# PEER decoder block: v rows half a block behind the u rows, two tokens in one product, and a block's last scaling one slot behind its sum and squares

## The chip, the cores and the metric

The kernel runs on one core of one Trainium2 chip, as one program. The metric is the device time of that program in microseconds (us), as a median of several runs; the kernel before takes 3320.57 us.

## What is computed

The reference is one decoder step for 1024 prompt tokens and 32 sample tokens of width 1024, all in float32. A first half mixes tokens (an input projection, causal pooling, a depthwise convolution of width 31, a LayerNorm, an output projection). The second half retrieves experts:

```python
q = (hf @ w_query).reshape(-1, PEER_HEADS, 2, PEER_HALF)
s = jnp.einsum('nhpk,hpmk->nhpm', q, sub_keys)
sv, si = lax.top_k(s, PEER_TOPK)                       # 16 of 128, twice a head
comb = sv[:, :, 0, :, None] + sv[:, :, 1, None, :]      # 256 pairs, the best 16 of them
fv, fpos = lax.top_k(comb.reshape(-1, 8, 256), PEER_TOPK)
...
a = jnp.einsum('phkd,pd->phk', u_table[ex], hx)        # 128 rows of u for every token
act = jax.nn.gelu(a, approximate=False) * gx
out = jnp.einsum('phk,phkd->pd', act, v_table[ex])     # 128 rows of v for every token
```

Each token takes 8 x 16 = 128 rows of `u_table` and the same 128 rows of `v_table`, 4 KB a row. For 1056 tokens that is 1109 MB of gathered rows. A residual add and a last RMSNorm follow.

## The kernel before

The tokens are 8 blocks of 128 and one of 32 (block `NB` = 8). The whole program is laid on a line of **slots**: (NB + 1) x 32 of them. In slot s = 32p + c, each engine's loop `for p ... for c ...` does chunk c of block p of the u part, chunk c of block p - 1 of the v part, and then the small steps that the table `steps[s]` names.

**The u part.** One u fetch is an indirect DMA issued by GpSimd (L783): pick k of all 128 tokens of the block, one row on each partition (512 KB). VectorE multiplies the row by the token and sums (L1337), one instruction of 1024 elements a fetch, four fetches a slot. The ring `u_ring` has NU = 6 places; a fetch waits until VectorE has freed its place (`u_free`). GpSimd also waits, each 32 picks, for `found`, the count of finished top-k searches (L777, inc at L1305).

**The v part.** One v fetch (L800) is the other way round: all 128 picks of one token, one on each partition. TensorE multiplies them (L1701) by a column of weights: `act_x` is a mostly zero buffer in which the weights of a token stand at such a distance that a window of 32 columns has them in the token's own row. The 128 tokens end up in the partitions of the two banks `acc`. Four v fetches a slot, ring `v_ring` with NV = 6 places, freed by TensorE (`v_free`). GpSimd issues in program order: four u fetches, then four v fetches, slot after slot.

**From u to v.** For the weights of a block all 128 picks must be done: VectorE `weigh(b)` multiplies gelu and gate to `act_w`, TensorE `weights(b)` transposes it (L1680), ScalarE `take_weights` copies it (L943), `spread` puts it into `act_x`, a quarter of the tokens at a time, and `tokens` (L1684) starts. This stands in slot 0 of the next block. The expert numbers are transposed likewise (`numbers`, `transposed_numbers`; table steps "turn", "turned"), once a block, since a v fetch needs all of a token's picks in one column. `finish(b)` (L1356) then scales the sums, adds y, squares and sums it (L1361 to L1366), waits for ScalarE's square root (L962) and scales (L1370), all in slot 0 of block b + 2.

**The table.** `lay_out()` (L157) fills `steps`: `fill` puts the token mixer and queries of the groups of blocks [2, 3, 4] and [5, 6, 7, 8] into slots by a list of costs (`COST`), from slot 5 on, up to a load per slot of 8 in block 0 and `ROOM` = 4.8 or 4.6 later; `spread` puts the pieces of the top-k searches. VectorE does a slot's steps one slot later (`DVE_LAG`). Group [0, 1] is worked ahead of slot 0. A step "xn" is `norm_x` (L1101) on VectorE, which waits for a square root by ScalarE (`x_root`, L835); "x" is the transposition on TensorE (`x_turned`, L1494), "in", "conv", "out", "q" are its products.

**Ends.** After slot 264 there is no u part; v fetches then use the places of both rings (`v_place`, `V_LAST`).

## Time and profile before

| | |
|---|---|
| three runs, us | 3320.57, 3324.29, 3314.8 |
| the profiled execution, us | 3321.2 |
| its span (first to last instruction), us | 3319.4 |
| mean granted TensorE clock, share of full | 0.82 |
| busy: TensorE / VectorE / ScalarE / GpSimd | 65% / 64% / 11% / 69% |
| moved by DMA | 1235.06 MB, 372 GB/s over the span |

The span is 1.8 us less than the execution's own time. A row of a timeline gives start, duration, engine, line, operation and tiles; in square brackets stands how long the engine had been idle and what ended that. A row of a table of stretches gives the stretch, its length, for each engine busy time and number of instructions, the granted clock, the DMA share and GB/s. CUSTOM_DVE_ANT_0 at L1337 is the u product; the trace's line numbers are those of the kernel before.

### The profile page before, as it was taken

What the parts mean: (1) busy time and instruction counts of PE and PEld (TensorE: products, weight loads), DVE (VectorE), ACT (ScalarE), POOL (GpSimd) and SP (SyncE); (2) the same over time, 40 slices, a digit from 0 to 9 for tenths busy, and PEclk for the clock granted to TensorE, in tenths of its full rate; (3) what the DMA queues carried; (4) which work ended last, traced back from release to release, by engine and by line L of the source; (5) the groups of instructions that cost most, each with busy time, mean ns of one, the idle gap of its engine ahead of it and who ended that gap; (6) DMA issues with size and microseconds to landing.
All of it is one profiled execution on the core that took longest, in us unless ns stands there. A gap on an engine that the chain in (4) does not pass through costs nothing.

```text
span 3319.4 us, 30349 instructions
## 1 busy us (share of the span) xinstructions
PE 2172.9 (65%) x9719; PEld 962.3 (29%) x9719; DVE 2132.8 (64%) x4860; ACT 360.3 (11%) x754; POOL 2284.6 (69%) x2229
## 2 busy tenths in 40 slices
PE   7884966567675588987564876674454445545576
PEld 5573532134331134542111443341111111111111
DVE  1577885767888557655756678777766666675301
ACT  2112340000001101321000000000000000000000
POOL 0144657677777777777767777777777777777675
PEclk9997988778887799999777887887666776786799
DMA  8778779999999999999999999999999999999998
GB/s 289 200 276 288 279 255 379 399 401 386 381 400 395 385 402 407 409 392 391 400 391 387 402 387 367 386 362 378 398 409 406 409 388 406 403 408 370 373 408 329
DMA packets 363454, 1235.06 MB, mean 372 GB/s; under 512 B 36856, under 2 KB 40336, under 8 KB 363280
## 3 DMA queue, kind: packets, MB, share of 16 engines
q0 software_dynamic: 304784, 1109.40, 86.7%
q1 hardware_dynamic: 36335, 79.69, 6.9%
q10 hardware_dynamic: 22176, 44.04, 3.5%
q8 instruction: 78, 1.28, 0.2%
q14 instruction: 81, 0.66, 0.1%
HBM read 1220.31 MB, written 13.28 MB: 372 GB/s over the span
## 4 chain that ended last, share of the span: by engine, by line
POOL 31%; DMA 26%; PE 22%; issue 11%; DVE 7%; DVEq 1%; ACT 1%; SPq 0%; POOLq 0%; ACTq 0%
DMA v_ring<-in_v_table_dram,eidt 19%; POOL u_ring L783 16%; POOL v_ring L800 14%; PE bank L1701 12%; DMA u_ring<-in_u_table_dram,eid 3%; PE bank L1520 3%; DVE u_ring L1337 2%; PE bank L1619 2%; PE bank L1537 2%; PE bank L1595 2%; DMA u_ring<-in_v_table_dram,eidt 1%; POOL u_ring L800 1%; DVE mixt L1176 1%; DMA wring<-in_w_in_dram 1%; DMA u_ring<-in_w_ada_dram 0%
## 5 line engine op out<-in xcount | busy, mean ns | idle before, releaser
L1701 PE MATMUL bank<-v_ring,act_x 128*32 128x512 f32 x3984 | 1165.9, 810 | 918.1 <-DMA v_ring<-in_v_table_dram,eidt 910.5
L1337 DVE CUSTOM_DVE_ANT_0 u_ring<-u_ring,h 128x1024 f32<-128x1024 f32 x1056 | 1278.4, 1225 | 745.3 <-DMA u_ring<-in_u_table_dram,eid 674.1
L783 POOL DMA_INDIRECT u_ring<-in_u_table_dram,eid x1024 | 1132.9, 1106 | 465.3 <-issue 302.8
L800 POOL DMA_INDIRECT v_ring<-in_v_table_dram,eidt x996 | 1041.4, 1046 | 392.0 <-issue 244.2
L1701 PEld LDWEIGHTS bank<-v_ring,act_x 128*32 128x32 f32 x3984 | 268.5, 135 | 1735.1 <-issue 1720.3
L1619 PEld LDWEIGHTS bank<-hbuf,wring 128*128 128x128 f32 x1984 | 230.1, 196 | 24.9 <-issue 24.9
L1619 PE MATMUL bank<-hbuf,wring 128*128 128x128 f32 (+1 forms) x1984 | 236.3, 280 | 0.0
L1537 PE MATMUL bank<-zc,dring 128*128 128x384 f32 x496 | 189.5, 508 | 7.7 <-ACT dring L832 7.7
L1520 PE MATMUL bank<-hbuf,wring 128*128 128x384 f32 (+2 forms) x448 | 151.4, 497 | 17.7 <-DMA wring<-in_w_in_dram 13.5
L1595 PE MATMUL bank<-wring,mixt 128*128 128x512 f32 (+1 forms) x256 | 125.0, 638 | 0.0
L1361 DVE TENSOR_TENSOR scratch<-bank,mod 128x512 f32<-128x512 f32 x18 | 11.6, 686 | 176.1 <-PE bank L1701 174.6
L1520 PEld LDWEIGHTS bank<-hbuf,wring 128*128 128x128 f32 x448 | 86.0, 195 | 85.4 <-issue 46.8
L1537 PEld LDWEIGHTS bank<-zc,dring 128*128 128x128 f32 x496 | 84.0, 190 | 55.4 <-issue 23.6
L832 ACT ACTIVATE dring<-ident,cw 128x128 f32<-128x128 f32 x248 | 78.4, 390 | 109.0 <-PE bank L1539 78.4
L1337 DVE DVE_READ_ACCUMULATOR2_ANT dot<- 128x1 f32 x1056 | 87.5, 83 | 0.0
L937 ACT ACTIVATE dot<-dot 128x32 f32<-128x32 f32 x33 | 7.6, 229 | 712.9 <-DVE dot L1337 696.3
L1701 PE MATMUL bank<-u_ring,act_x 128*32 128x512 f32 x240 | 57.3, 595 | 22.6 <-DMA u_ring<-in_v_table_dram,eidt 22.6
L800 POOL DMA_INDIRECT u_ring<-in_v_table_dram,eidt x60 | 56.2, 937 | 21.3 <-issue 15.6
L1595 PEld LDWEIGHTS bank<-wring,mixt 128*128 128x128 f32 (+1 forms) x256 | 47.0, 192 | 79.8 <-issue 79.8
L916 ACT ACTIVATE qt<-bank 128x512 f32<-128x512 f32 (+1 forms) x36 | 20.2, 562 | 366.6 <-PE bank L1619 366.6
L927 ACT ACT_TABLE_LOAD x32 | 41.1, 1283 | 166.5 <-PE bank L1595 92.1
L1539 PEld LDWEIGHTS bank<-zcs,dring 128*128 128x128 f32 x248 | 46.9, 189 | 33.1
(260 smaller groups left out, 1679.6 us busy)
## 6 DMA issues: line engine op xcount, KB each, us to landing
u_ring<-in_u_table_dram,eid POOLq DMA_INDIRECT x1024, 7.1
wring<-in_w_out_dram ACTq DMA_DIRECT2D x16, 1024.0 KB, 11.7
wring<-in_w_query_dram ACTq DMA_DIRECT2D x16, 1024.0 KB, 11.6
v_ring<-in_v_table_dram,eidt POOLq DMA_INDIRECT x996, 7.5
wring<-in_w_in_dram ACTq DMA_DIRECT2D x10, 1024.0 KB, 11.7
xr<-in_x_prompt_dram SPq DMA_DIRECT2D x16, 512.0 KB, 7.3
v_ring<-in_w_ada_dram SPq DMA_DIRECT2D x7, 1024.0 KB, 13.5
wring<-in_w_ada_dram SPq DMA_DIRECT2D x5, 1024.0 KB, 5.4
```

The lines of the kernel that those rows point to most:

```text
L783: pool.indirect_dma_start(u_ring[:, n % NU], None, u_table[0], bass.IndirectOffsetOnAxis(ap=col, axis=0)).then_inc(u_in[n % NU], 16)
L800: pool.indirect_dma_start(place, None, v_table[0], bass.IndirectOffsetOnAxis(ap=eidt[:, b % RING, t:t + 1], axis=0)).then_inc(landed, 16)
L832: last = act.activation(diag_at(g, c, j), ident[:, :], ACT.Copy, scale=cw[:, j, c:c + 1])
L927: act.activation(g, g, ACT.Exp).then_inc(exp_ready, 1)
L1176: last = dve.scalar_tensor_tensor(out=m, in0=z, scalar=w, in1=m, op0=ALU.mult, op1=ALU.add)
L1337: dve.tensor_tensor_reduce(u_ring[:, n % NU], u_ring[:, n % NU], h2[:, b % 2], 1.0, 0.0, ALU.mult, ALU.add, dot[:, b % 2, k:k + 1]).then_i ...
L1520: last = pe.matmul(ps[PROJ[c]][:, 0:n], w[:, k, c * P:(c + 1) * P], h1t[:, h * HK + k, 0:n], start=(h + k == 0), stop=(h * HK + k == KC - 1))
L1537: last = pe.matmul(ps[2 + c % 2][:, 0:np], diag_at(g, c, j), zc[:, c, j:j + np], start=(j == 0), stop=(j == CK - 1))
L1539: last = pe.matmul(ps[7][:, c * S:(c + 1) * S], diag_at(g, c, j), zcs[:, c, :, j:j + TS], start=(j == 0), stop=(j == CK - 1))
L1595: last = pe.matmul(bank, mixt[:, h * HK + k, t0:t0 + n], w[:, k, :], start=False, stop=(h * HK + k == KC - 1))
L1619: last = pe.matmul(q_bank(b)[:, a * n:(a + 1) * n], w[:, k, a * P:(a + 1) * P], h2_cols(b)[:, h * HK + k, :], start=(h + a + k == 0), stop ...
L1701: last = pe.matmul(acc[h][j * S:(j + 1) * S, :], act_x[:, i % 2, j, a:a + S], v_place(n)[0][:, h * HALF:(h + 1) * HALF], start=(c == 0), s ...
```

## The change

The v part of a block no longer waits for all its 128 picks but for the first 64. A constant `LAG` = 16 slots is the distance of v behind u, where it was 32. A v fetch now brings, for **two** tokens (q and q + 16 of a group of 32), 64 picks each: token q on partitions 0 to 63, token q + 16 on partitions 64 to 127. In the first 16 slots of a block's v part all 128 tokens are done with picks 0 to 63, in the second 16 with picks 64 to 127, both summed into the same `acc`. So fetches, bytes and products of the v part are as many as before: 128 fetches a block, 8 products (32x512) a slot. What comes twice a block instead of once: `weigh`, `weights`, `take_weights`, the transposed numbers. In `act_x`, column 0 holds the weights of the first token and column 16 those of the second, so each `spread` is two ScalarE instructions of 64 partitions.

```diff
+LAG = NCH // 2
+HK2 = H * K // 2
-ROOM = [None, 4.8, 4.6]
+ROOM = [None, 6.6, 6.4]
...
-            while load[at] >= (room if at >= NCH else 8):
+            while load[at] >= (room if at >= LAG else 8):
+                load[at + 1] += load[at] - (room if at >= LAG else 8)
                 at += 1
...
-    at = 5
+    at = 2
     for g in range(1, NG):
...
             def v_fetch(b, i):
                 n = b * P + i
-                if i == 0:
-                    pool.wait_ge(eidt_ready, b + 1)
+                h, pair_no = divmod(i, HK2)
+                if pair_no == 0:
+                    pool.wait_ge(eidt_ready, 2 * b + h + 1)
...
-                t = S * (i % 4) + i // 4 if b < NB else i
+                t = HK2 * h + 16 * (pair_no % 4) + pair_no // 4 if b < NB else i
...
-                    for j in range(CH):
-                        if p:
-                            v_fetch(p - 1, c * CH + j)
-                    if p == 0 and c == NCH // 2:
+                    if v_chunk(p * NCH + c):
+                        b, vc = v_chunk(p * NCH + c)
+                        for j in range(CH):
+                            v_fetch(b, vc * CH + j)
+                    if p == 0 and c == LAG - 3:
                         pool.wait_ge(mod_taken, 12)
                         pool.memset(act_x[:, :, :, :], 0.0)
...
                     if p and c == 0:
-                        weigh(p - 1)
-                    if p > 1 and c == 0:
-                        finish(p - 2)
+                        weigh(p - 1, 1)
+                    if p < NB and c == LAG:
+                        weigh(p, 0)
+                    if p and c == LAG:
+                        take_sums(p - 1)
+                        add_sums(p - 1)
+                    if p and c == LAG + 1:
+                        finish(p - 1)
...
             for p in range(NB + 1):
                 for c in range(NCH):
-                    if p:
-                        if c == 0:
-                            weights(p - 1)
-                        tokens(p - 1, c)
+                    if v_chunk(p * NCH + c):
+                        b, vc = v_chunk(p * NCH + c)
+                        if vc % LAG == 0:
+                            weights(b, vc // LAG)
+                        tokens(b, vc)
+                    if p == NB and c == NSG + 2:
+                        weights(NB, 0)
```

`v_chunk(s)` is `divmod(s - LAG, NCH)`. `take_sums` and `add_sums` are the first two parts of the old `finish` (L1356 to L1366), `finish` now only its last (L1367 to L1370); they stand in slots 16 and 17 of block b + 1. Table steps "turn" and "turned" come twice a block. The SyncE transfers of y stand in slot 20 instead of slot 3. The weights of the sample block are made in slot 266 instead of after the loop.

The table `steps` that results differs in most slots by a few. Three places matter below. **VectorE, block 0, after the fourth chunk of u products.** Before, the norm of x for the next group (L1116 to L1109, two blocks) comes after the seventh chunk:

```order
L1337 ISA dot 128x1
L1116 COPY zc<-zc 128x4x30
L1117 COPY zp<-zp 128x4x15
L1105 ISA scratch,sst<-xr 128x1024
L1105 ISA sst 128x1
L1107 RECIPROCAL sst<-sst 128x1
L1109 TENSOR_SCALAR xr<-xr,sst 128x1024
```

In the change the same rows (its lines are 29 higher) come after the fourth chunk, and a third norm follows after the sixth:

```order
L1375 ISA dot 128x1
L1145 COPY zc<-zc 128x4x30
L1146 COPY zp<-zp 128x4x15
L1134 ISA scratch,sst<-xr 128x1024
L1134 ISA sst 128x1
L1136 RECIPROCAL sst<-sst 128x1
L1138 TENSOR_SCALAR xr<-xr,sst 128x1024
```

**TensorE, second half of block 0.** Before, the convolution of group [2, 3, 4] runs without v products between:

```order
L1520 MATMUL bank<-hbuf,wring 128x384 x96
L1537 MATMUL bank<-zc,dring 128x384 x47
L1649 MATMUL bank<-ident,eidf 128x128
L1537 MATMUL bank<-zc,dring 128x384 x77
L1554 MATMUL bank<-zp,wpn 128x384
```

In the change it is spread over slots 15 to 26, between the v products (L1762) of block 0, which begin with the transposed weights (L1740):

```order
L1573 MATMUL bank<-hbuf,wring 128x384 x60
L1590 MATMUL bank<-zc,dring 128x384 x16
L1740 MATMUL bank<-ident,act_w 64x128 x2
L1762 MATMUL bank<-v_ring,act_x 32x512 x8
L1590 MATMUL bank<-zc,dring 128x384 x8
L1762 MATMUL bank<-v_ring,act_x 32x512 x8
L1590 MATMUL bank<-zc,dring 128x384 x7
```

**GpSimd, block 0.** Before, the first v fetches follow 132 u fetches:

```order
L783 DMA u_ring<-in_u_table_dram,eid 128x1024 x68
L814 MEMSET act_x 128x2240
L783 DMA u_ring<-in_u_table_dram,eid 128x1024 x64
L800 DMA v_ring<-in_v_table_dram,eidt 128x1024 x4
```

In the change they follow 68, and the clearing of `act_x` stands three slots earlier:

```order
L801 DMA u_ring<-in_u_table_dram,eid 128x1024 x56
L836 MEMSET act_x 128x2240
L801 DMA u_ring<-in_u_table_dram,eid 128x1024 x12
L821 DMA v_ring<-in_v_table_dram,eidt 128x1024 x4
```

## Rows read from the trace of the kernel before

**Rows 1.** Page, part 2: busy tenths and GB/s in 40 slices of 83 us.
```profile
DMA  8778779999999999999999999999999999999998
GB/s 289 200 276 288 279 255 379 399 401 386 381 400 395 385 402 407 409 392 391 400 391 387 402 387 367 386 362 378 398 409 406 409 388 406 403 408 370 373 408 329
```

**Rows 2.** Table of stretches: block 0 in quarters, then u and v together.
```profile
core 0: us, PE busy (x) PEld busy (x) DVE busy (x) ACT busy (x) POOL busy (x), PEclk, DMA share, GB/s
196.00:272.00 76.00, 57.86 (x555) 54.87 (x553) 61.10 (x139) 11.82 (x20) 42.43 (x33) 0.91 0.98 366
272.00:349.00 77.00, 43.95 (x124) 25.63 (x125) 60.08 (x148) 16.82 (x36) 43.36 (x32) 0.76 0.82 277
349.00:425.00 76.00, 70.22 (x217) 40.42 (x216) 60.92 (x133) 29.44 (x84) 46.55 (x34) 1.00 0.78 265
425.00:497.00 72.00, 49.50 (x143) 27.52 (x142) 65.53 (x138) 29.34 (x68) 40.73 (x33) 0.87 0.73 252
497.00:884.00 387.00, 252.36 (x1138) 112.27 (x1139) 272.83 (x689) 25.34 (x42) 286.38 (x256) 0.82 1.01 390
```

**Rows 3.** The same table, slots 99 to 113.
```profile
1302.00:1456.00 154.00, 151.85 (x704) 83.38 (x702) 99.12 (x193) 42.96 (x125) 116.42 (x120) 1.00 1.03 409
```

**Rows 4.** Lines L783 and L800: duration min/median/max, first and last start.
```profile
L783 POOL DMA_INDIRECT u_ring<-in_u_table_dram,eids x32: 933/952/1797, 3037.8 to 3119.0; - x32
...
L800 POOL DMA_INDIRECT v_ring<-in_v_table_dram,eidt x996: 932/938/2503, 502.2 to 3285.7; - x200
L800 POOL DMA_INDIRECT u_ring<-in_v_table_dram,eidt x60: 933/937/940, 3150.8 to 3296.1; - x60
```

**Rows 5.** Timeline, VectorE, GpSimd and TensorE: slot 16 and slots 31 to 32.
```profile
365.85 1.22 DVE L1337 CUSTOM_DVE_ANT_0 u_ring<-u_ring,h 128x1024 f32<-128x1024 f32 x1
...
497.22 0.94 POOL L783 DMA_INDIRECT u_ring<-in_u_table_dram,eid  x1 [13.94 <-DVEq L1305]
...
501.63 1.23 DVE L1337 CUSTOM_DVE_ANT_0 u_ring<-u_ring,h 128x1024 f32<-128x1024 f32 x1 [4.71 <-DMA u_ring<-in_u_table_dram,eid]
...
510.40 0.47 PE L1680 MATMUL bank<-ident,act_w 128*128 128x128 f32 x1 [25.55 <-DVEq L1354]
```

**Rows 6.** Timeline, four engines and SyncE's queue: the norm of x in block 0.
```profile
235.62 0.08 DVE L1337 DVE_READ_ACCUMULATOR2_ANT dot<- 128x1 f32 x1
...
255.62 0.60 ACT L922 ACTIVATE s_mem<-bank 128x512 f32<-128x512 f32 x1 [1.25 <-PE bank L1635]
...
259.15 1.08 PE L1477 MATMUL bank<-mod,y 128*32 128x128 f32 x32 [0.81 <-DMA mod<-in_w_ada_dram]
...
268.47 21.17 SPq L569 DMA_DIRECT2D xr<-in_x_prompt_dram  x3
...
271.86 0.94 POOL L783 DMA_INDIRECT u_ring<-in_u_table_dram,eid  x1 [10.10 <-DVEq L1305]
...
287.32 1.97 PE L1503 MATMUL bank<-ident,xr 128*128 128x128 f32 x8 [16.68 <-DVE xr L1109]
...
293.51 6.73 PE L1520 MATMUL bank<-hbuf,wring 128*128 128x384 f32 x14 [4.22 <-ACT hbuf L845]
```

**Rows 7.** Timeline, slots 224 to 227: u products and transfers of SyncE.
```profile
2701.66 1.22 DVE L1337 CUSTOM_DVE_ANT_0 u_ring<-u_ring,h 128x1024 f32<-128x1024 f32 x1 [5.28 <-DMA u_ring<-in_u_table_dram,eid]
...
2715.75 0.34 SPq L601 DMA_DIRECT2D out_dram<-y  x1
...
2719.95 2.68 SPq L593 DMA_DIRECT2D h<-h_scratch  x4
...
2739.90 1.23 DVE L1337 CUSTOM_DVE_ANT_0 u_ring<-u_ring,h 128x1024 f32<-128x1024 f32 x1 [2.33 <-DMA u_ring<-in_u_table_dram,eid]
```

**Rows 8.** Table of stretches, the u fetches at L783 alone.
```profile
196.00:349.00 153.00, 85.78 (x64) 0.83 0.90 321
349.00:497.00 148.00, 85.30 (x65) 0.94 0.75 259
...
2750.00:3019.00 269.00, 102.48 (x104) 0.73 1.02 405
```

More of the change, by code:

```diff
@@ L119, in top_steps @@
         out += [("top", *x, j) for j in range(max(1, first_piece(x[1])), 3)] + [("nrm", *w) for w in was]
-        last = [w[1] for w in was if w[0] == PARTS - 1]
-        out += [("turn", b) for b in last] + [("top", *x, i) for i in range(3, PIECES)] + [("turned", b) for b in last]
+        half = [(w[1], w[0] // 2) for w in was if w[0] % 2 and w != (1, SB)]
+        out += [("turn", *h) for h in half] + [("top", *x, 3)] + [("turned", *h) for h in half] + [("top", *x, 4), ("top", *x, 5)]
     b = todo[-1][1]
-    return out + [("gap", 1), ("exp", *todo[-1]), ("turn", b), ("gap", 1), ("nrm", *todo[-1]), ("gap", 1), ("turned", b)]
+    return out + [("gap", 1), ("exp", *todo[-1]), ("turn", b, 1), ("gap", 1), ("nrm", *todo[-1]), ("gap", 1), ("turned", b, 1)]
 def mixer_steps(g):
@@ L198, in spread @@
             last = int(at)
+            if i[0] == "turn" and last % LAG > LAG - 5:
+                last = at = last // LAG * LAG + LAG
             slots[last].append(i)
@@ L404, in build, with halves, v_chunk @@
         DVE_LAG = 1
-        SPREAD_AT = (0, 1, 10, 18)
-        turned = [sum(1 for s_ in range((p + 1) * NCH) for step in steps[s_] if step[0] == "turn") for p in range(NB + 1)]
+        SPREAD_AT = (0, 1)
+        turned = [sum(1 for s_ in range(LAG * (i + 1)) for step in steps[s_] if step[0] == "turn") for i in range(2 * NB)]
+        turned.append(2 * NB + 1)
+        def halves(s):
+            return min(s // LAG, 2 * NB)
+        def v_chunk(s):
+            return divmod(s - LAG, NCH) if 0 <= s - LAG < NB * NCH else None
         def s_at(part, b):
@@ L698, in _ @@
                     h2_load(p + 1)
-                if s % NCH == 3 and p >= 2:
-                    y_store(p - 2)
-                    y_load(p - 1)
+                if s % NCH == LAG + 4 and 0 < p < NB:
+                    y_store(p - 1)
+                    y_load(p)
             y_store(LAST)
@@ L1285, in piece @@
                         key_top(part, b, 3)
+                    if (part, b) == (PARTS - 1, 0):
+                        dve.drain().then_inc(s0_used, 1)
                     dve.tensor_copy(sif[:, :, :], best(part, b)[1])
@@ L1640, in scores, with numbers @@
                 last.then_inc(s_ps, 1)
-            def numbers(b, p):
-                pe.wait_ge(found, TOP_NO[PARTS - 1, b] + 1)
-                if b:
-                    pe.wait_ge(eidt_ready, b)
-                if p:
-                    pe.wait_ge(act_taken, p)
-                n = rows(b)
-                pe.transpose(ps[6][:, 0:n], eidf[0:n, b % 3, :], ident[0:n, 0:n]).then_inc(eidt_ps, 1)
+            def numbers(b, h, s):
+                pe.wait_ge(found, TOP_NO[2 * h + 1, b] + 1)
+                if b + h:
+                    pe.wait_ge(eidt_ready, 2 * b + h if b < NB else 2 * b)
+                if halves(s):
+                    pe.wait_ge(act_taken, halves(s))
+                if b < NB:
+                    for a in range(2):
+                        last = pe.matmul(ps[6][a * HK2:(a + 1) * HK2, 0:P], eidf[:, b % 3, h * HK2:(h + 1) * HK2], ident[:, :], start=True, stop=True)
+                else:
+                    last = pe.transpose(ps[6][:, 0:S], eidf[0:S, b % 3, :], ident[0:S, 0:S])
+                last.then_inc(eidt_ps, 1)
             def states_turned():
@@ L1672, in states_out, with weights @@
                 last.then_inc(st_ps, 1)
-            def weights(b):
-                pe.wait_ge(act_ready, b + 1)
-                pe.wait_ge(eidt_ready, turned[min(b, LAST)])
-                if b:
-                    pe.wait_ge(act_taken, b)
+            def weights(b, h):
+                i = 2 * b + h
+                pe.wait_ge(act_ready, i + 1)
+                pe.wait_ge(eidt_ready, turned[i])
+                if i:
+                    pe.wait_ge(act_taken, i)
                 if b < NB:
-                    pe.transpose(ps[6][:, P:2 * P], act_w[:, :], ident[:, :]).then_inc(act_ps, 1)
+                    for a in range(2):
+                        last = pe.matmul(ps[6][a * HK2:(a + 1) * HK2, P:2 * P], act_w[:, h * HK2:(h + 1) * HK2], ident[:, :], start=True, stop=True)
+                    last.then_inc(act_ps, 1)
                 else:
@@ L1761, in _ @@
                 for c in range(NCH):
-                    if p:
-                        if c == 0:
-                            weights(p - 1)
-                        tokens(p - 1, c)
+                    if v_chunk(p * NCH + c):
+                        b, vc = v_chunk(p * NCH + c)
+                        if vc % LAG == 0:
+                            weights(b, vc // LAG)
+                        tokens(b, vc)
+                    if p == NB and c == NSG + 2:
+                        weights(NB, 0)
                     for step in steps[p * NCH + c]:
@@ L1790, in _ @@
                         elif kind == "turn":
-                            numbers(step[1], p)
+                            numbers(*step[1:], p * NCH + c)
                         elif kind == "state_out":
                             states_out(step[1])
-            weights(NB)
             for c in range(NSG):
```

84 lines of the change are left out of this document (51 added, 33 removed).

## Prediction

> **What bounds the kernel now.** The page's slices come first [rows 1]: after the sixth slice of 83 us the DMA engines are at 9 tenths to the end, near 400 GB/s; before it they are at 7 or 8, with 255 to 289 GB/s for slices four to six. The table of stretches [rows 2] says the same by block. While block 0's u rows run alone (196 to 497 us), the last two quarters move 265 and 252 GB/s; as soon as u and v rows run together (497 to 884) it is 390. The best stretch [rows 3] has 15 slots of 8 fetches in 154 us, 10.27 us a slot, at 409 GB/s; 8 fetches of 512 KB are 4.19 MB, and 4.19 MB at 409 GB/s are 10.25 us. That is the floor of a slot, and TensorE with a convolution and v products (151.85 of 154 us busy) still keeps to it. So the kernel is bound by DMA from slot 32 on, and by its chains of engines in block 0: there a slot takes (501.63 - 365.85) / 16 = 8.5 us [rows 5] for half the fetches. At slot 32 nothing flows: GpSimd sat 13.94 us until the top-k search of block 1 ended, and TensorE 25.55 us until VectorE had the weights of block 0 [rows 5].
>
> **What the change does to that.** It removes nothing from the stream; it moves 64 v fetches from the end, where they stand alone, into slots 16 to 31 of block 0, where the DMA engines have room. I go by one profiled execution of 3321.2 us (span 3319.4), 0.6 us above the median of the three runs.
>
> *The end: -86 us.* The last u fetch starts at 3119.0, the last v fetch at 3296.1 [rows 4]. Between them are the 4 v fetches of slot 263, 24 slots of 4, and 32 of the sample block: 132 fetches in 177.1 us, 1.34 us each. After the change v is 16 slots nearer, so 64 of them are gone: 64 x 1.34 = 86 us. What follows the last fetch (23 us) stays. The weights of the sample block are made earlier, which saves nothing that shows, since the fetches here hardly stop for it.
>
> *Slots 16 to 31: +40 us.* They take 136 us now [rows 5] and carry 8 fetches instead of 4 afterwards. Lower bound: the floor, 16 x 10.25 = 164 us. To it comes the other traffic: between 349 and 497 us about 38.3 MB moved (76 us at 265 GB/s, 72 at 252), of which 64 u fetches are 33.6 MB; the 4.7 MB left are 12 us at 409 GB/s. Together 176 us, so +40. Upper bound: the price of block 1, where products, norms and searches are dense, 387 us for 32 slots [rows 2], 12.1 a slot, 194 us, so +58. I take 176, because these slots hold the convolution in pieces of 8 products beside 8 v products, which is what stands in the best stretch [rows 3]; TensorE's clock was 1.00 there, its higher level (2.4 GHz), and 1.00 and 0.87 in the two quarters here [rows 2]. The wait of GpSimd at slot 32 is inside the 136 us; afterwards 4 v fetches stand ahead of the waiting one, and no norm comes between the search's last two pieces, so I let 3 us go from the first slots of block 1: **-3**.
>
> *The start: +11 us.* The mixer begins at slot 2 instead of 5, so VectorE reaches the norm of x after its fourth chunk, at 235.7 us [rows 6]. The norm squares (1.2 us) and waits for ScalarE's root. ScalarE runs its program in order and has taken the last scores of group [0, 1] only at 256.2 [rows 6]. So VectorE will stand from about 237 to 256.5, some 19 us, and behind it stand its u products, the search of picks 32 to 63 and with it the u fetches of slot 8, which now start at 271.86. The third norm needs x loaded into the place of the first, and SyncE may load only after TensorE's transposition, which cannot come before 260.2 (its modulation ends then); it will be there when asked. All 19 us come before the search of picks 32 to 63 is done, so the u fetches of slot 8 start at about 290, 18 us late. Some comes back: TensorE's projection, which now starts at 293.51 after waits of 16.68 and 4.22 us [rows 6], starts some 7 us sooner, because its third x is normed two slots of VectorE earlier. Between 0 (all made good, since the later slots of this half have waits of their own) and +18 I take +11.
>
> *Hand-overs: +10 us.* Each time the v part goes to new weights, TensorE waits for VectorE, v fetches fill the six places and GpSimd stops behind them, the u fetches too. Slots 224 to 226 show one: 2701.66 to 2739.90 is 38.2 us [rows 7] against 30.8 at the floor, 7.5 over. Three transfers of 512 KB belong to it (y out, y in, tokens in), 3.8 us at 409 GB/s; 3.7 us is the stall. There were 8 such, now there are 16. But the last scaling goes to the next slot, the root's wait is hidden by searches, and the other eight have no sums. I put 2.5 us on each: 16 x 2.5 - 8 x 3.7 = +10. The lower bound is 0 (the places of the ring cover all), the upper 16 x 7.5 - 8 x 7.5 = +60.
>
> *At nothing:* the second transposition of numbers, ScalarE's doubled spreads (256 ns become two of about that, on an engine busy 11%), the rearranged slots of groups 1 and 2. If SyncE is late with y, nobody waits: y is used 28 slots later.
>
> Sum: -86 + 40 - 3 + 11 + 10 = -28, 3321.2 - 28 = 3293.
>
> **A rule that speaks against it.** The u fetches of block 0's second half took 83.3 us for 64 (85.30 less one clearing of 1.98 us), 1.30 us each; between 2750 and 3019 us 104 took 102.48, 0.99 each [rows 8]. So GpSimd needs 0.3 us more a fetch when VectorE is dense, and sits 0.30 us between two. At 1.60 us, 8 fetches are 12.8 us and no longer under the floor. The Trainium skill, page "SBUF — State Buffer", section "SBUF: two separate sides", says that GpSimd cannot write the descriptors of its own DMAs while VectorE holds the port they share. By that rule GpSimd would set the pace there, which is the second rival; the trace agrees that fetches under dense VectorE work are longer.
>
> **The rivals.**
> 1. *The hand-over costs in full, 16 times.* Place: TensorE's `weights`, slots 0 and 16 of every block. Price 7.5 instead of 2.5 us each and no gain from the split: +60 instead of +10, 3343, **slower**. It decides from about +47, that is 5.9 us for each of the 8 new ones. For it: 25.55 us of TensorE's wait at the first one, and six places that six fetches fill in 8 us. Against: transfers make half of the 7.5. Chance 0.13.
> 2. *GpSimd is the bound in slots 16 to 31.* 16 x 12.8 = 205 instead of 176: +29, 3322, no change. For: rows 8. Against: in the best stretch VectorE was 64% busy and fetches kept the floor; 390 GB/s in block 1. Chance 0.14.
> 3. *The start and the hand-overs are covered.* +0 for both: 3272, faster. For: ring places and slack of VectorE. Chance 0.20.
> 4. *It does not do what it says:* the early v rows only push work of block 0 later, so that these slots and the next 16 run like the worst block and the freed DMA time is not used: +58 instead of +40, and 16 slots more at 0.9 us over today's, +14: 3325. Chance 0.07.
>
> My forecast has 0.46.
>
> **How the numbers follow.** A measurement of this kernel tells about 0.3% from no change, so faster is below 3311, slower above 3331. Faster: nearly all of the forecast (0.44), rival 3 (0.20), a part of rival 2 (0.02): 0.66. Slower: rival 1 (0.12), a part of 2 and 4 (0.05): 0.17. The rest 0.17. The range goes from 3262 (rival 3, with the slots at 166 us) to 3328 (rivals 2 and 4); outside are rival 1 and some 6 in 100 below.
>
> **What would show it.** The slice of 332 to 498 us should rise from 250 to 280 GB/s to near 400. Slot 32's u products should start at about 550 us (501.63 + 48). VectorE should show one wait of near 19 us for the root at about 237 us. From the last u fetch to the last v fetch should be 91 us instead of 177. Hand-overs should show TensorE waits of some 5 us without GpSimd standing over 2 us. I am wrong if slots 16 to 31 take over 195 us, or if the eight later blocks take over 15 us more than now.

## The result, and the profile after

The change takes 3361.28 us (median of 4 runs, 3353.78 to 3364.71) against 3321.34 us of the kernel before beside it: ratio 1.012, 95% interval 1.0096 to 1.0144. It is slower; the forecast was 3293 us, its range ended at 3328. The profiled execution is the quickest of these four: its span of 3352.0 us is 32.6 over that of before, while the medians differ by 39.9. What follows accounts for the 32.6.

The page of the kernel after, part 2, as [rows 1]:

```profile
DMA  8778799999999999999999999999999999999998
GB/s 290 202 256 273 285 375 365 381 387 396 402 367 389 384 368 403 381 346 387 385 394 393 375 384 392 388 383 385 345 392 409 400 406 406 406 383 399 377 376 326
```

Slice 6 rose from 255 to 375 GB/s, as meant. Slices 7 to 29, where nothing was meant to change, are lower in 15 of 23 places: 365 instead of 379, 381 instead of 399, 387 instead of 401.

To see where the time went I cut both spans at the first u product of slots 0, 16, 32, 192 and 256. The table of stretches, kernel before (us of the stretch, busy time and instructions of each engine, granted clock, DMA share, GB/s):

```profile
205.60:365.85 160.25, 113.55 (x687) 85.54 (x688) 128.52 (x322) 28.78 (x55) 85.96 (x63) 0.84 0.90 320
365.85:501.63 135.78, 102.87 (x307) 58.16 (x305) 112.75 (x226) 57.27 (x150) 83.19 (x64) 0.91 0.74 252
501.63:2365.90 1864.27, 1285.49 (x5782) 576.12 (x5784) 1303.90 (x3134) 194.54 (x392) 1391.68 (x1283) 0.83 1.01 391
2365.90:3042.43 676.53, 336.14 (x1035) 78.98 (x1031) 443.68 (x882) 30.45 (x49) 510.79 (x511) 0.70 1.02 401
3042.43:3319.39 276.96, 174.03 (x645) 40.22 (x643) 56.34 (x92) 6.71 (x14) 185.91 (x189) 0.87 0.96 368
```

The same of the kernel after:

```profile
205.43:385.65 180.22, 126.28 (x723) 91.93 (x724) 129.19 (x324) 32.15 (x66) 87.36 (x68) 0.83 0.85 298
385.65:571.50 185.85, 150.23 (x530) 63.62 (x529) 109.47 (x225) 45.28 (x134) 132.38 (x124) 0.93 0.94 353
571.50:2478.48 1906.98, 1277.32 (x5862) 576.29 (x5862) 1318.59 (x3165) 205.66 (x423) 1411.08 (x1283) 0.82 0.99 383
2478.48:3159.08 680.60, 332.71 (x1062) 77.50 (x1058) 444.85 (x888) 33.17 (x59) 510.47 (x511) 0.73 1.01 399
3159.08:3351.98 192.90, 108.09 (x393) 25.16 (x391) 51.62 (x88) 4.20 (x12) 124.13 (x125) 0.83 0.92 349
```

Row by row the change costs +20.0, +50.1, +42.7 and +4.1 us and gains 84.1, which makes 32.8. The gain is the forecast one. The third row is the surprise: 160 slots take 42.7 us more for the same fetches, at 383 instead of 391 GB/s. No engine is busier by as much there (VectorE +14.7, GpSimd +19.4, TensorE 8.2 less), but GpSimd's part is to be kept in mind: it is the engine that issues every row.

The end, as [rows 4]: from the last u fetch to the last v fetch are 95 us, where 177 were.

```profile
L801 POOL DMA_INDIRECT u_ring<-in_u_table_dram,eids x32: 934/938/979, 3154.5 to 3233.7; - x32
...
L821 POOL DMA_INDIRECT u_ring<-in_v_table_dram,eidt x30: 932/937/941, 3259.7 to 3328.7; - x30
```

The start, as [rows 6] (timeline of the kernel after: start, duration, engine and line, idle time before and what ended it):

```profile
256.26 0.16 DVE L1136 RECIPROCAL sst<-sst 128x1 f32<-128x1 f32 x1 [20.34 <-ACT sst L860]
...
266.20 1.68 POOL L801 DMA_INDIRECT u_ring<-in_u_table_dram,eid  x1 [28.24 <-DVE dot L1375]
...
280.74 1.97 PE L1556 MATMUL bank<-ident,xr 128*128 128x128 f32 x8 [19.80 <-DVE xr L1138]
...
299.53 2.90 PE L1573 MATMUL bank<-hbuf,wring 128*128 128x384 f32 x4 [16.82 <-ACT hbuf L867]
```

VectorE's wait for the root came as forecast: 20.34 us. GpSimd stood 28.24 us behind it for a free u place, and slot 8 began 19.2 us later than before (298.33 for 279.17). But the projection, which I had starting 7 us sooner than 293.51, started 6 us later. TensorE now waits 16.82 us for `hbuf`: the third x of the group stands on ScalarE in slot 7 behind the gelu of block 0's first part, which wants the u products of chunk 7.

A hand-over in the middle, slot 80, timeline of the kernel after, TensorE and GpSimd:

```profile
1163.82 0.94 POOL L821 DMA_INDIRECT v_ring<-in_v_table_dram,eidt  x1 [0.30 <-issue]
1171.80 1.95 POOL L821 DMA_INDIRECT v_ring<-in_v_table_dram,eidt  x1 [7.04 <-PE bank L1762]
...
1166.54 0.69 PE L1740 MATMUL bank<-ident,act_w 128*64 128x128 f32 x4 [12.31 <-DVEq L1396]
1168.17 3.43 PE L1762 MATMUL bank<-v_ring,act_x 128*32 128x512 f32 x16 [0.93 <-ACT act_x L980]
```

and VectorE before it writes the weights (L1385), which TensorE waits for:

```profile
1158.90 1.22 DVE L1375 CUSTOM_DVE_ANT_0 u_ring<-u_ring,h 128x1024 f32<-128x1024 f32 x1
...
1160.22 0.29 DVE L1264 MAX8 s_mem<-dring 128x8 f32<-128x128 f32 x1
...
1165.87 0.46 DVE L1164 COPY zcs<-bank 128x120 f32<-128x120 f32 x2
1166.24 0.21 DVE L1385 TENSOR_TENSOR act_w<-dot,gate 128x64 f32<-128x64 f32 x1
```

The products of the slot are done at 1160.1, but a search over scores (from 1160.22) and copies of the sample states (to 1166.2) stand ahead of the weights in VectorE's program. TensorE stands 12.31 us, v fetches fill the six places, and GpSimd stands 7.04 us. While it stands nobody asks for rows. The waits of GpSimd (us in total, times, longest) for the slots 32 to 255 sum this up, kernel before:

```profile
POOL v_ring L800 <- PE bank L1701: 135.4, 182, 8.6
```

and after:

```profile
POOL v_ring L821 <- PE bank L1762: 163.2, 193, 9.1
```

Counting only GpSimd's stands over half a microsecond, and each for the slot in which it begins, they rise there from 108 to 136 us. In the slots 16k and 16k + 1 (two in sixteen) they rise from 19 to 42 us, in all others from 89 to 94. So 23 of 29 us of standing lie where the v part changes its weights. The stretch itself grew by 46.8 us; another 19 are fetches that kept GpSimd busy longer, and what made them longer is not shown.

### The profile page after: what moved, and what is told of

It reads as the page before. It is cut to its first block, busy times and chain, and to the rows that moved or that the text cites. A ratio compares the mean times of both kernels' runs of the same rounds, so it can differ in the third digit from the quotient of the medians.

```text
span 3352.0 us, 30694 instructions
## 1 busy us (share of the span) xinstructions
PE 2155.3 (64%) x9831; PEld 957.7 (29%) x9831; DVE 2141.3 (64%) x4892; ACT 363.0 (11%) x788; POOL 2292.5 (68%) x2229
## 4 chain that ended last, share of the span: by engine, by line
POOL 31%; PE 24%; DMA 24%; issue 11%; DVE 7%; DVEq 1%; ACT 1%; SPq 0%; POOLq 0%; ACTq 0%
DMA v_ring<-in_v_table_dram,eidt 18%; POOL u_ring L801 15%; POOL v_ring L821 15%; PE bank L1762 12%; PE bank L1672 4%; DMA u_ring<-in_u_table_dram,eid 4%; DVE u_ring L1375 2%; PE bank L1590 2%; PE bank L1648 2%; PE bank L1573 2%; DMA wring<-in_w_out_dram 1%; DMA u_ring<-in_v_table_dram,eidt 1%; DVE mixt L1205 1%; DVE work L1266 0%; PE bank L1688 0%
## 5 line engine op out<-in xcount | busy, mean ns | idle before, releaser
L1762 PE MATMUL bank<-v_ring,act_x 128*32 128x512 f32 x4104 | 1167.5, 809 | 950.6 <-DMA v_ring<-in_v_table_dram,eidt 932.5
L801 POOL DMA_INDIRECT u_ring<-in_u_table_dram,eid x1024 | 1115.2, 1089 | 455.5 <-issue 305.4
L821 POOL DMA_INDIRECT v_ring<-in_v_table_dram,eidt x1026 | 1097.2, 1069 | 436.9 <-issue 249.7
L1762 PEld LDWEIGHTS bank<-v_ring,act_x 128*32 128x32 f32 x4104 | 268.9, 135 | 1751.9 <-issue 1725.9
L1590 PE MATMUL bank<-zc,dring 128*128 128x384 f32 x496 | 197.0, 521 | 8.9 <-ACT dring L854 8.9
L1404 DVE TENSOR_TENSOR scratch<-bank,mod 128x512 f32<-128x512 f32 x18 | 11.6, 686 | 95.2 <-PE bank L1762 93.7
L1740 PE MATMUL bank<-ident,act_w 128*64 128x128 f32 x64 | 10.1, 410 | 92.2 <-DVEq L1396 92.2
L944 ACT ACTIVATE dring<-bank 128x512 f32<-128x512 f32 x28 | 16.7, 597 | 375.5 <-PE bank L1688 287.8
## 6 DMA issues: line engine op xcount, KB each, us to landing
wring<-in_w_query_dram ACTq DMA_DIRECT2D x16, 1024.0 KB, 11.6
```

The lines of the kernel that those rows point to most:

```text
L801: pool.indirect_dma_start(u_ring[:, n % NU], None, u_table[0], bass.IndirectOffsetOnAxis(ap=col, axis=0)).then_inc(u_in[n % NU], 16)
L821: pool.indirect_dma_start(place, None, v_table[0], bass.IndirectOffsetOnAxis(ap=eidt[:, b % RING, t:t + 1], axis=0)).then_inc(landed, 16)
L1590: last = pe.matmul(ps[2 + c % 2][:, 0:np], diag_at(g, c, j), zc[:, c, j:j + np], start=(j == 0), stop=(j == CK - 1))
L1762: last = pe.matmul(acc[h][j * S:(j + 1) * S, :], act_x[:, i % 2, j, a:a + S], v_place(n)[0][:, h * HALF:(h + 1) * HALF], start=(c == 0), s ...
```

## The experiments

My theory after this: the third row's 43 us come from the **table** of slots, which carries work over and fills single slots with up to 11.5 units; the start's 20 us from the norms. Rivals: the **lag** or the **hand-overs** themselves. The runs stood on chips of two speeds: in some groups of runs the kernel before takes 3318 to 3321 us, as above ("the faster chip" below), in others 3523 to 3527 ("the slower chip"). Every ratio is to the kernel before in the same group. The chip number 0 stands beside both speeds (3526 and 3527 us in two groups, 3320 in a later one), so whether the speed belongs to the piece or to its state at the time is not shown. The kernel before was profiled only at 3320 us.

**On the slower chip.** *norms_later* takes the change and moves four steps:

```diff
+    for item, a, z in ((('xn', 3), 2, 4), (('xn', 2), 2, 4), (('x', 2), 4, 5), (('xn', 4), 4, 6)):
+        slots[a].remove(item)
+        slots[z].insert(0, item)
```

> The changed kernel with only the first norms of group [2, 3, 4] put later in block 0: xn of blocks 2 and 3 from slot 2 to 4, x of block 2 from slot 4 to 5, xn of block 4 from slot 4 to 6. Theory 'start' (VectorE's 20.3 us wait for the root is lost time, and the projection's 16.8 us wait for ScalarE too): that wait falls under 3 us, slot 8 starts some 16 us earlier, slot 16 10 to 20 us earlier, and the whole is 3341 to 3351 us. Rival 'absorbed' (the time comes back before slot 32, since DMA and TensorE set it): slot 32 at the same 570 us and the whole 3356 to 3363.

Measured: 1.0048 (1.0015 to 1.0082), where the unaltered change took 1.0105 in a later group. Slot 8 began at 279.6 us and slot 16 at 371.1, in the change 298.3 and 385.7. So the wait at the start is worth some 14 us, as the theory 'start' said. The idle time before the line of the root is 6.0 us in all; in the change it is 23.2:

```profile
L1139 DVE RECIPROCAL sst<-sst x9: 150/164/164, 17.7 to 1262.3; 128x1 f32<-128x1 f32 x8, 32x1 f32<-32x1 f32 x1
its engine sat idle before it (us, times) until:
  ACT sst L863: 6.0, 8
```

*old_table_new_lag* is the change with the old table:

```diff
-ROOM = [None, 6.6, 6.4]
+ROOM = [None, 4.8, 4.6]
-            while load[at] >= (room if at >= LAG else 8):
-                load[at + 1] += load[at] - (room if at >= LAG else 8)
+            while load[at] >= (room if at >= NCH else 8):
-    at = 2
+    at = 5
```

> The changed kernel with the table of before: mixer from slot 5, ROOM 4.8 and 4.6, no carry of overload, so that only the half block of lag, the two tokens in one product and the split finish are left. Theory 'table' (the 42 us lost between slots 32 and 192 come from the new filling of slots, which makes overfull ones): slots 32 to 192 take 1865 us as before, the start is as before, and the whole is 3285 to 3305 us. Rival 'hand-overs' (they come from TensorE's second wait per block in slots that it fills): slots 32 to 192 still take 1895 to 1910, the whole is 3325 to 3345.

*new_table_old_lag* is the kernel before with these lines the other way (`NCH // 2` for `LAG`).

> The kernel before with the filling rule of the change alone: mixer from slot 2, ROOM 6.6 and 6.4, carry of overload; v a whole block behind u, one hand-over a block. Theory 'table': +18 us at the start, +35 to 45 in slots 32 to 192, the whole 3370 to 3385 us. Rival 'hand-overs': only the start is lost, 3333 to 3343 us.

*halves_old_lag* has all of the change, but v rows a whole block behind:

```diff
+DLY = NCH
-            return divmod(s - LAG, NCH) if 0 <= s - LAG < NB * NCH else None
+            return divmod(s - DLY, NCH) if 0 <= s - DLY < NB * NCH else None
-                    if p and c == 0:
-                        weigh(p - 1, 1)
-                    if p < NB and c == LAG:
-                        weigh(p, 0)
+                    if p and c == 0:
+                        weigh(p - 1, 0)
+                    if p and c == LAG:
+                        weigh(p - 1, 1)
```

(and sums, y and spreads placed to match).

> The changed kernel with v a whole block behind u again, but everything else kept: two tokens in one product, 16 hand-overs, split finish, the new table. Against new_table_old_lag it prices hand-overs and halves without the lag. Theory 'table': within 8 us of new_table_old_lag. Rival 'hand-overs': 25 to 40 us slower than new_table_old_lag. Against the changed kernel it prices the lag: both theories 35 to 50 us slower than the change (86 us of lone v fetches come back, 50 us of slots 16 to 31 go).

Measured: old_table_new_lag 0.9944 (0.9917 to 0.9971), new_table_old_lag 1.0133 (1.0075 to 1.0191), halves_old_lag 1.0133 (1.0073 to 1.0192). So on this chip lag and halves with the old table gain half a per cent, and the new table without them costs 1.3. Two hand-overs a block, on the new table, changed the median by 2 us; the four runs of each kernel spread over 17 and 18 us, so a cost of some ten would not be seen. Against change_again the lag was worth 0.3%, some 10 us by the ratios, not the 35 to 50 expected.

Then the table was taken apart. *change_again* is the change unaltered. *late_start_carry*: the change with `at = 5` and `NCH` for `LAG` in the rule. *early_start_no_carry*: `at = 2`, the rest of the table old. *early_light_no_carry*: as that, and the bound holds from `LAG` on.

> The change unaltered, on the chip of the next three runs, as their measure. Both theories: 1.012 of the kernel before as measured, or up to 1.015 on a chip whose DMA is slower, since the table of slots was worth 1.013 by itself on such a chip.

> The change with group 1 starting at slot 5 and slots up to 31 held to 8 as before, but with the new bounds 6.6 and 6.4 and the excess carried over. Theory A (the carry rule, which puts up to 11.5 of work into one slot, costs in slots 32 to 191 and the early norms cost at the start): the start's 24 us come back and the 45 us of the later slots stay, 1.005 to 1.008. Theory B (the early start and the light slots 16 to 31 cost, the carry nothing): 0.995. Theory C (any table that is not the old one costs, by chance meetings of bursts): near 1.005 too, but then the next two runs cost as much.

> The change with the old bounds 4.8 and 4.6, nothing carried and slots up to 31 held to 8, only the start at slot 2 is new. Theory A: the old table's gain less the 20 to 24 us at the start: 1.000 to 1.002. Theory B: 1.006 or more, since slots 0 to 15 hold 100 units of work instead of 65. Theory C: 1.010 to 1.015 (start and table).

> As the run before, and the bound of 4.8 holds from slot 16 on: the new table but for carry and bounds (61 units of work in slots 16 to 31 instead of 93). Theory A: slots 16 to 31 some 5 us shorter and nothing else, 0.999 to 1.002. Theory B: as the change, 1.010 to 1.012. Theory C: 1.010 to 1.015.

Measured: 1.0105 (1.0068 to 1.0142), 1.0102 (1.0069 to 1.0135), 1.0067 (1.0037 to 1.0097), 1.007 (1.0044 to 1.0096). Slots 32 to 191 took 2035 and 2042 us with carrying, 1993 and 2006 without, 1981 in old_table_new_lag. Theory A was right in kind, but the tables without carry stayed 0.7% over: my estimate of 1.000 to 1.002 put the early start too low. The late start with carry came out at 1.010, not 1.005 to 1.008, although its slots 0 to 15 took 161.7 us where the change took 181.2. One kernel's executions lie up to 1.4% apart on this chip, so only the larger of these differences carry weight.

*old_table_again* repeats old_table_new_lag. *piled_conv* adds to it

```diff
+    for s in (98, 100, 102, 104, 106, 108, 110):
+        moved = [i for i in slots[s + 1] if i[0] == 'conv']
+        slots[s + 1] = [i for i in slots[s + 1] if i[0] != 'conv']
+        slots[s] += moved
```

and *carry_capped* is the change with

```diff
-            while load[at] >= (room if at >= LAG else 8):
-                load[at + 1] += load[at] - (room if at >= LAG else 8)
+            while load[at] >= (room if at >= LAG else 8) or at >= 96 and load[at] + cost(i) > 8.7:
+                load[at + 1] += max(0, load[at] - (room if at >= LAG else 8))
```

> The change with the table of the kernel before (start at slot 5, 8 up to slot 31, bounds 4.8 and 4.6, nothing carried), once more, as the measure of the next three. All theories: 0.994, as on the chip before (0.9917 to 0.9971), with slots 32 to 191 near 1980 us and 0 to 31 near 367.

> As the run above, but seven times in slots 98 to 111 the convolution step of the second slot of a pair is done in the first, 11.5 units beside none, where before each had 5.8. Theory A (an overfull slot makes the work of a slot longer than the six places of the ring cover, so GpSimd stops and the DMA engines lose what is not made up): some 4 us a pile, the stretch of slots 96 to 111 28 us longer than above (near 222 instead of 194 us), the whole 1.002. Theory C (the sum of the work counts, where it stands does not): 0.994, the stretch within 5 us.

> The change with its table, but from slot 96 on no step is put where it makes a slot fuller than 8.7: 106, 155, 164 and 173 (11.5, 8.8, 8.8, 8.8) are gone, six slots of 8.6 or 8.8 before 99 stay. Theory A: slots 96 to 191 near 1190 us as in the tables without carry (1184 and 1195) instead of the change's 1214, so 1.004 to 1.006. Theory C: as the change, 1.0105, slots 96 to 191 at 1210 or more.

> Look at the table that is light in slots 16 to 31 and carries nothing, a second time, to see how far one kernel's stretches repeat between executions: slots 32 to 191 within 10 us of 2006, the start (slots 0 to 31) within 3 of 382, the waits of GpSimd over half a microsecond near 244 us. If they do not repeat so, no stretch difference under 20 us may be read as a cause.

(The last is one execution of early_light_no_carry, with nothing moved; its name misleads.) Measured: 0.996 (0.9938 to 0.9982), 1.005 (1.0027 to 1.0074), 1.0072 (1.0047 to 1.0096). The repeated execution had slots 32 to 191 within 8 us (1998 for 2006) and GpSimd's stands, counted as above, within 5 (224 for 219 us), but slots 0 to 31 took 393 for 382; so of the stretches between executions on the slower chip I read nothing under some 15 us. Table of stretches, slots 96 to 111, of old_table_again:

```profile
1373.04:1561.12 188.08, 170.08 (x737) 87.04 (x733) 110.86 (x212) 48.71 (x144) 136.25 (x127) 0.99 0.98 365
```

and of piled_conv:

```profile
1362.88:1593.65 230.77, 171.68 (x733) 91.09 (x729) 110.83 (x212) 46.74 (x140) 130.81 (x129) 0.90 0.80 300
```

TensorE does the same work (170 and 172 us), in 43 us more time: 6 us for each pile, where 4 were expected. One pile in the timeline of piled_conv, GpSimd:

```profile
1438.32 0.94 POOL L825 DMA_INDIRECT v_ring<-in_v_table_dram,eidt  x1 [0.30 <-issue]
1456.96 0.94 POOL L825 DMA_INDIRECT v_ring<-in_v_table_dram,eidt  x1 [17.70 <-PE bank L1766]
```

and TensorE, which begins the two convolution steps 9.56 us late because the diagonal tiles of both come from ScalarE in one piece:

```profile
1445.02 1.62 PE L1594 MATMUL bank<-zc,dring 128*128 128x384 f32 x2 [9.56 <-ACT dring L858]
```

The two products of that row take 1.62 us; before the wait two such took 0.89, and from 1451 us on they do so again. The granted clock was 0.92 from 1429 to 1436 us, 0.50 (the lower level, 1.2 GHz) from 1445 to 1450, and 1.00 from 1451 to 1455. So a part of a pile's cost is TensorE's clock after its stand. GpSimd stood 17.7 us until TensorE had left the convolution and freed a v row. The 80 slots behind took 992.8 us, where they took 996.6 without piles, so hardly anything was made up. carry_capped moved one 11.5 and three 8.8 away and slots 96 to 191 fell from 1214 to 1186 us; the whole, 1.0072, is not clear of the change's 1.0105, whose interval begins at 1.0068. So a slot over its measure costs; piled_conv shows it, on this chip.

**On the faster chip** *both_repaired* (early_light_no_carry with the four norm steps moved) should have given nearly all back.

> The change with its early start at slot 2 and its light slots 16 to 31, but nothing carried, bounds 4.8 and 4.6, and four steps moved so that VectorE no longer waits for the root of group 1's third norm at slot 2 (norms of 2 and 3 at slot 4, x of 2 at 5, norm of 4 at 6). If the loss is the sum of these two faults and nothing else: slots 0 to 31 near 362 us (382 to 391 less 20 to 24), slots 32 to 191 near 2002, the whole 0.996 to 0.999, that is 35 to 50 us under the change. If something else of the early start costs (work of group 1 in the same slots as block 0's search), slots 0 to 31 stay over 375 us and the whole is 1.003 or more.

It did not: 1.011 (1.0094 to 1.0126), against 1.012 of the change there. Slots 0 to 31 took 360 us, as expected with both faults repaired, but slots 32 to 191 took 1906.5, as in the change. My theory of two faults fell for the chip on which the change was measured. The next three runs go back to the first question, whether table or lag costs.

> The change with the table of the kernel before, which gave 0.994 and 0.996. If the table decides everywhere: 0.994 again, with slots 32 to 191 within 10 us of the kernel before on the same chip (1864 us where it takes 3320 in all). If the lag itself takes the 42 us there on a chip where the whole takes 3320: 1.004 or more, slots 32 to 191 near 1905.

> The kernel before with the change's table, lag as before. If the table decides: 1.011 to 1.013, slots 32 to 191 near 1905 us on a chip of 3320. If the lag does: 1.005 (the start's 20 us alone), slots 32 to 191 near 1865.

> The new table without carry and with four norm steps later, which gave 1.011 (slots 32 to 191: 1906.5 us, as the change). If it is a matter of the chip that carrying costs (the slower one, where nearly all of the runs stood): on the slower chip 0.997 to 1.001; on the faster one again 1.011.

Measured, again on the faster chip: 1.0008 (0.9995 to 1.0022), 1.0079 (1.0062 to 1.0095), 1.0103 (1.0085 to 1.0121). Neither the table alone nor the lag alone is it. both_repaired_2 is both_repaired a second time, and it shows how well stretches repeat on the faster chip: slots 0 to 15, 16 to 31, 32 to 191, 192 to 255 and the end are all within 2.2 us of the first (32 to 191: 1905.9 for 1906.5). Two last runs: *halves_old_table* (halves_old_lag with the old table) and *late_carry_2* (late_start_carry).

> The kernel before with its own table and with v rows a whole block behind as before, but two sets of weights a block, so 16 hand-overs instead of 8, and the last scaling a slot later. If hand-overs cost by themselves: GpSimd's stands at the hand-over slots of 32 to 255 rise from 19 us (kernel before) to 32 or more and the whole is 1.003 to 1.006. If they cost only together with the half block's lag or with the new table: 0.999 to 1.002.

> The change with the start at slot 5 and 8 up to slot 31, but the new bounds and the carrying. On a chip where the kernel before takes 3320: if carrying costs there as it did on the slower one (0.4 to 1.5%), slots 32 to 191 near 1905 us against 1877 of the old table, slots 96 to 111 near 190 against 172, the whole 1.008; if the early start is what costs there, 1.001 to 1.003.

Measured: 1.0065 (1.0047 to 1.0082) and 1.0066 (1.0047 to 1.0085). In the first, GpSimd's stands in the slots 16k and 16k + 1 rose from 19 to 31 us; the second was expected at 1.008 if carrying costs and at 1.001 to 1.003 if the early start does. The tables of stretches for slots 16 to 31, 32 to 191, 192 to 255 and the end; halves_old_table:

```profile
366.71:500.10 133.39, 103.66 (x310) 58.32 (x308) 112.86 (x227) 57.24 (x150) 81.74 (x62) 0.92 0.75 252
500.10:2377.92 1877.82, 1287.75 (x5854) 577.58 (x5856) 1308.17 (x3154) 201.90 (x417) 1407.50 (x1283) 0.83 1.00 388
2377.92:3065.53 687.61, 350.26 (x1058) 79.95 (x1056) 444.51 (x887) 31.77 (x58) 520.38 (x511) 0.70 1.01 395
3065.53:3342.66 277.13, 176.43 (x657) 41.36 (x653) 57.14 (x96) 8.37 (x20) 184.24 (x189) 0.84 0.96 368
```

old_table_third:

```profile
368.43:566.27 197.84, 153.92 (x570) 69.30 (x568) 115.76 (x228) 58.45 (x155) 132.69 (x124) 0.89 0.91 341
566.27:2443.48 1877.21, 1288.32 (x5852) 578.52 (x5854) 1312.40 (x3161) 202.34 (x418) 1398.43 (x1283) 0.83 1.00 389
2443.48:3131.56 688.08, 342.83 (x1060) 78.16 (x1058) 444.69 (x887) 33.05 (x59) 517.19 (x511) 0.74 1.01 394
3131.56:3324.46 192.90, 110.03 (x397) 25.74 (x393) 51.76 (x88) 4.20 (x12) 122.88 (x125) 0.81 0.92 349
```

new_table_old_lag_2, slots 32 to 191:

```profile
503.70:2387.75 1884.05, 1280.84 (x5792) 574.71 (x5794) 1308.92 (x3138) 199.27 (x398) 1398.01 (x1283) 0.83 1.00 387
```

late_carry_2, slots 32 to 191:

```profile
553.89:2465.76 1911.87, 1283.28 (x5860) 576.97 (x5862) 1318.77 (x3164) 205.48 (x423) 1407.41 (x1283) 0.82 0.99 382
```

These make a ladder from before to after in three rungs, each a difference of rows.

1. *Two sets of weights a block (with two tokens in one product and the scaling a slot later), old lag, old table:* slots 32 to 191 +13.6, 192 to 255 +11.1; **+25**. The four slots from each 16k on (14 places, slots 32 to 255) take 23.8 us more in sum, so it lies at the hand-overs: 15.6 at the seven new ones, 8.2 at the seven old ones. GpSimd's stands are no longer in sum (107 us for 108), since others fell; it was busy 25.4 us longer over the same fetches (15.8 and 9.6 in the two rows). So the place of the 25 us is shown, the way they come about is not.
2. *v rows half a block nearer:* slots 16 to 31 +64.5, the end -84.2, between them -0.1 (-0.6 and +0.5); **-20**. This is what the change is for, and it works.
3. *The new table on that:* slots 0 to 15 +16.6, 16 to 31 -12.0, 32 to 191 +29.8, 192 to 255 -7.5; **+27**. Of the 29.8, 19.9 lie in slots 96 to 111, which hold the convolution of the last group and the slot of 11.5 units (106).

Slots 96 to 111 of old_table_third and of the change:

```profile
1337.09:1508.92 171.83, 163.71 (x734) 86.56 (x732) 110.68 (x211) 49.00 (x144) 132.55 (x128) 1.00 1.02 403
1348.42:1540.14 191.72, 176.15 (x752) 91.88 (x750) 112.17 (x215) 46.56 (x136) 135.80 (x128) 0.96 0.96 367
```

GpSimd's waits for v places are 7.5 us in the first and 21.8 in the second, with one of 9.1 us right behind slot 106. Here the mechanism of the pile shows on the faster chip too.

25 - 20 + 27 = 32, and the spans differ by 32.6. By medians of all runs the rungs are +23, -19 and +36, together 40, the last between two groups of runs. On the faster chip rung 1 ate what rung 2 gave. On the slower one lag and halves together gained 0.56% and 0.4% (0.9944, 0.996), which is what rung 2 alone would give (20 of 3525 us is 0.57%); that rung 1 costs nothing there was seen only on the new table, within the spread named above.

Within rung 3, late_carry_2 shows carrying without the early start: 1911.9 instead of 1877.2 us for slots 32 to 191, but 9.6 us less in 16 to 31 and 7.0 less in 192 to 255. Its slots 96 to 111 take 188.3 us against 171.8 of the old table. So the new bounds with carrying cost there without the early start (1.0066, where the old table gave 1.0008). both_repaired_2 has no carrying, and its slots 96 to 111 take 179 us, yet slots 32 to 191 still take 1905.9: its stands of GpSimd at slots 48 and 80 are 10.3 and 11.9 us, in the old table 5.2 and 0. That without carrying other bursts met hand-overs is my reading of these two; no run separates it.

No kernel here beats the one before on both chips; old_table_new_lag is 0.4 to 0.6% faster on the slower and the same on the faster. Not tried, and open: weights placed ahead of the slot's searches in VectorE's program, which by the rows of slot 80 would free TensorE some 6 us sooner.

## Why the prediction was wrong

Step by step, for the chip on which the change was measured:

- *What bounds the kernel:* right in the number, not shown in the cause. The floor of 10.25 us a slot was put down to DMA at 409 GB/s. In the kernel before, slots 196 to 219 go by undisturbed, 10.32 us each (table of stretches, then GpSimd's waits):

```profile
2413.05:2660.68 247.63, 122.63 (x387) 29.58 (x385) 157.36 (x305) 11.10 (x16) 188.75 (x193) 0.69 1.02 408
POOL u_ring L783 <- issue: 29.3, 96, 0.3
POOL v_ring L800 <- issue: 28.1, 92, 0.3
```

  GpSimd is busy 188.75 us and rests 0.3 us after each fetch (57.4 us, and 1.5 more at five fetches): together 247.65, the whole stretch. It never waits for a place, so here its own issuing sets the pace, while the DMA engines are at a share of 1.02 as well. No run separates the two. The prediction had the numbers in its rows 8: 0.99 + 0.30 us, eight times, is 10.3 us. Either way nothing is left to catch up with after a stand.
- *The end, -86:* right, 84.1 us.
- *Slots 16 to 31, +40:* +50.1. The sum "floor plus other traffic" takes 409 GB/s; 353 were reached. It was the size that was off, by two things of opposite sign: in the old table the same step cost 62 us (197.8 against 135.8), near the +58 that I had as the upper bound, and the light new table gave 12 back.
- *Slot 32, -3:* the 16 slots from 32 on took 2.4 us less.
- *The start, +11:* +20.0. The wait of VectorE was right to a microsecond or two. The discount was wrong: "TensorE's projection starts some 7 us sooner" ignored ScalarE, where the third x now stands behind a gelu.
- *Hand-overs, +10:* +25 (rung 1). I priced eight new ones at 2.5 us, which is near the 2.2 measured (15.6 / 7), but let the old ones fall by 1.2 each through the split scaling; they rose by 1.2. TensorE waited 7.1 us each time (92.2 us in 13), near the 5 expected, but GpSimd stood up to 8.3 us at one (slot 64), not under 2.
- *"At nothing: the rearranged slots of groups 1 and 2":* **the step that failed.** It is +30 us in slots 32 to 191, and +20 (1884.05 against 1864.27) already without the lag. The prediction gave no reason for the term beyond its first one, that DMA bounds the kernel from slot 32 on. But such a cover holds only while GpSimd keeps asking. An estimate from the rows: six v places are a slot and a half of the stream, some 15 us, and half of that goes for landing (the median from issue to landing of the v rows is 7.2 us); a burst of TensorE or VectorE longer than the rest stops GpSimd, which has no time of its own to make it up with. In slots 96 to 111, where two thirds of the loss lie, the rows above show this; for the other third it is not shown.

With the measured sizes the prediction's own sum is -84 + 50 + 20 + 47 = +33 instead of -28 (47 is 42.7 + 4.1, slot 32, hand-overs and table together). The miss of the profiled execution is 61 us, of the medians 68. Of the 61 some 24 are in slots 0 to 31, at slot 32 and at the end, some 15 are the hand-overs, some 22 the table (rung 3 less its parts in slots 0 to 31).

Of its signs of being wrong, slots 16 to 31 over 195 us did not come (185.9); the eight later blocks over 15 us more did (46.8).

Rival 1, hand-overs at 7.5 us each, named the right place and side but not the price: +25, and it decides from +47. Rival 2, GpSimd as the bound at 12.8 us a slot in slots 16 to 31, had the price wrong, for the slots took 11.6 in the change and 12.4 with the old table. The engine it named is not cleared: there GpSimd was busy 132.4 us of 185.9 and rested 0.3 us after 115 fetches, which is nine tenths of the time, and waited 18.7 us for places or the search. A run with fewer or larger fetches would decide it, and none was made. The rule cited with it (the Trainium skill, page "SBUF — State Buffer", section "SBUF: two separate sides") says that GpSimd cannot write descriptors while VectorE holds their port. The trace does not speak against it, since single fetches of 1.95 us stand beside the usual 0.94, but no run here shows that VectorE's port makes them so. Rival 4 foresaw loss in the next 16 slots; slots 32 to 47 took 2.4 us less than before.

The chances failed by a habit: three terms were each taken near their kind end, and the rivals let only one go wrong at a time. No rival held the term that failed.

## What to carry to other kernels

Where a stream is at its limit, or its issuer has no time of its own left, and each slot shares it with a program of other work, a term "at nothing" needs the ring's depth beside the longest burst of the new order, not the sum of the work. Moving bytes from a bare end into a half-idle start pays the difference of the two marginal prices (here 84 against 64 us), and that small rest is easily eaten by hand-overs. Before calling a stream bound by DMA, add up the issuing engine's busy time and its rests: here they fill the quickest slots. Change the lag and the table in separate steps, and measure in more than one group of runs, since a gain of 0.5% in one was nothing in another.

## What the runs showed that was not expected

The two chip speeds differ unevenly. The change in slots 192 to 255 on the slower one:

```profile
2629.70:3375.50 745.80, 350.44 (x1058) 77.20 (x1056) 443.39 (x887) 33.15 (x59) 543.64 (x511) 0.71 0.97 364
```

against 680.60 us at 399 GB/s above, 9.6% more, while the whole kernel is 6% longer; in slots 96 to 111 the old table reached 403 GB/s on the faster and 365 on the slower. The median of these 64 slots is 11.35 us instead of 10.24, though the quickest take 10.2 on both. That fits a pace set by GpSimd's issuing on the faster chip, with the DMA engines behind it on the slower one. Why hand-overs cost 25 us on the faster chip and no more than the spread on the slower is not explained. On the slower GpSimd stood 268 us in slots 32 to 191 of new_table_old_lag, where the same kernel stood 108 us on the faster one, and a stand at one place may replace one at another. Both are only argued.
